# Eight layer normalisations with the sum of squares, root and reciprocal on tokens in the partitions

## What is computed

```python
def layer_norm(x, g=None, b=None):
    x32 = x.astype(jnp.float32)
    mu = jnp.mean(x32, axis=-1, keepdims=True)
    xc = x32 - mu
    y = xc * lax.rsqrt(jnp.mean(xc * xc, axis=-1, keepdims=True) + LN_EPS)
    if g is not None:
        y = y * g + b
    return y.astype(x.dtype)

def first_block(x, c, ...):
    ...
    h = layer_norm(x) * (1.0 + sc_m) + sh_m
    mix = hybrid_mixer(h, ...)
    x = layer_norm(DEEPNORM_ALPHA * x + g_m * mix, ln_mix_g[l], ln_mix_b[l])
    h = layer_norm(x) * (1.0 + sc_f) + sh_f
    ffn = grouped_moe(h, ...)
    x = layer_norm(DEEPNORM_ALPHA * x + g_f * ffn, ln_ffn_g[l], ln_ffn_b[l])

def second_block(x, c, ...):
    for i in range(2):
        ...
        x = layer_norm_2(ALPHA * x + (1.0 + gate) * y, ln_mix_g[i], ln_mix_b[i])
        ...
        x = layer_norm_2(ALPHA * x + (1.0 + gate) * y, ln_ffn_g[i], ln_ffn_b[i])
    return x
```

## Time and profile before

| | us |
|---|---|
| median of three runs | 4085.99 |
| lowest and highest run | 4078.77 and 4087.83 |
| span of the profiled execution | 4087.4 |
| TensorE busy | 3216.4 |
| VectorE busy | 1877.5 |
| ScalarE busy | 885.8 |

### The profile page before, as it was taken

How to read it: one execution, slowest core, us unless ns; L and a number is a source line. 1 busy time by engine, 2 the same in 40 slices (tenths; PEclk the granted TensorE clock), 3 DMA queues, 4 the chain that set the end, 5 groups by cost and what they waited for, 6 DMA issues and landing times. The chain is left out here.

```text
span 4087.4 us, 33743 instructions
## 1 busy us (share of the span) xinstructions
PE 3216.4 (79%) x11149; PEld 1986.0 (49%) x11149; DVE 1877.5 (46%) x2996; ACT 885.8 (22%) x1338; POOL 336.7 (8%) x405
## 2 busy tenths in 40 slices
PE   4699998769988888669995697899843555578998
PEld 3355556544444466434442345678631111257786
DVE  7465463425565524411113444433418888644333
ACT  1211112212222232211112132413210000223132
POOL 0000000000000000010000000000005777000000
PEclk6677678879999988779997788899976777799999
DMA  7453432121111031069883001323020000114220
GB/s 270 124 154 108 123 108 83 61 84 52 35 32 36 0 124 41 1 223 325 311 325 136 28 16 42 124 87 99 21 49 3 0 0 0 41 41 134 93 93 31
DMA packets 305892, 373.55 MB, mean 91 GB/s; under 512 B 31720, under 2 KB 234011, under 8 KB 305820
## 3 DMA queue, kind: packets, MB, share of 16 engines
q1 hardware_dynamic: 298508, 346.92, 26.0%
q0 software_dynamic: 4000, 13.64, 0.9%
q10 hardware_dynamic: 3312, 12.06, 0.7%
HBM read 356.32 MB, written 16.27 MB: 91 GB/s over the span
## 5 line engine op out<-in xcount | busy, mean ns | idle before, releaser
L451 PE MATMUL banks<-mlp_h_parts,mlp_w_parts 128*128 128x512 f32 x1536 | 357.7, 396 | 57.0 <-DVE mlp_w_parts L439 57.0
L451 PEld LDWEIGHTS banks<-mlp_h_parts,mlp_w_parts 128*128 128x128 f32 x1536 | 294.1, 192 | 121.4 <-DVE mlp_w_parts L439 59.5
L451 PE MATMUL banks<-mlp_hidden,mlp_w_parts 128*128 128x512 f32 x1536 | 348.8, 389 | 0.0
L2359 PE MATMUL banks<-h,s_scan_ck 128*32 128x512 f32 x256 | 181.4, 875 | 180.1 <-DVE h L2412 180.1
L451 PEld LDWEIGHTS banks<-mlp_hidden,mlp_w_parts 128*128 128x128 f32 x1536 | 288.3, 188 | 59.8
L439 DVE TENSOR_TENSOR mlp_w_parts<-w_second,mlp_w_parts 128x2048 fp32r<-128x2048 f32 x64 | 146.6, 2293 | 207.1 <-ACT mlp_w_parts L434 207.1
L1641 PE MATMUL banks<-w,experts_xt 128*128 128x512 f32 x544 | 239.0, 598 | 0.9 <-DVE experts_xt L1692 0.9
L2359 PEld LDWEIGHTS banks<-h,s_scan_ck 128*32 128x32 f32 x256 | 36.0, 153 | 324.2 <-DVE h L2412 208.2
L434 ACT ACTIVATE mlp_w_parts<-w_second 128x2048 fp32r<-128x2048 f32 x64 | 122.3, 1913 | 249.0 <-PE banks L451 245.8
L1641 PEld LDWEIGHTS banks<-w,experts_xt 128*128 128x128 f32 x544 | 104.3, 192 | 132.6 <-issue 132.6
L761 DVE SCALAR_TENSOR_TENSOR attention_mod_sum<-w,silu_c,attention_mod_sum 128x256 f32<-128x256 f32 x336 | 162.9, 485 | 12.0
(11 more groups left out here) (550 smaller groups left out, 5148.4 us busy)
## 6 DMA issues: line engine op xcount, KB each, us to landing
w_second<-in_mlp_w_dram SPq DMA_DIRECT2D x64, 1024.0 KB, 5.5
w<-in_w_exp_gate_dram SPq DMA_DIRECT2D x17, 2048.0 KB, 9.4
w<-in_w_exp_up_dram SPq DMA_DIRECT2D x17, 2048.0 KB, 9.2
w<-in_w_exp_down_dram SPq DMA_DIRECT2D x17, 2048.0 KB, 11.0
w<-in_w_ada_dram SPq DMA_DIRECT2D x12, 2048.0 KB, 8.5
w<-in_mod_mix_w_dram SPq DMA_DIRECT2D x24, 1024.0 KB, 9.5
w<-in_mod_ffn_w_dram SPq DMA_DIRECT2D x24, 1024.0 KB, 5.2
w<-in_w_in_dram SPq DMA_DIRECT2D x32, 512.0 KB, 5.5
```

Source lines behind the costliest of these rows:

```text
L451: mm = pe.matmul(out, self.parts[:, n % 2, w, kk, f * P:(f + 1) * P], x[:, v, kk, :], start=(start and kk == 0 and j == 0), stop=(stop and ...
L2359: mm = pe.matmul(ps[rows, 4, :], ck[:, r, 32 * j:32 * j + 32], pr[:, j % 2, n, :], start=(n == 0), stop=(n == 3))
```

## The change

Only `norm_stage` is changed, and with it all eight normalisations. The square tiles become the stationary operand, in blocks of 128 channels by 128 tokens, and one column of ones the moving one. The sum of squares of a token so comes out with tokens on the partitions, one column for each block of 128 tokens, in the banks 1 to 4. Root and reciprocal are taken on 128x4. Four products of 128 columns then bring the result back to the form with tokens in the free dimension and the same value on all partitions: the stationary operand is a column of `rstd` broadcast to 128 columns, the moving one the identity, and the result goes to bank 5, from where VectorE reads it as it scales the tiles. The wait of VectorE for its own reciprocal becomes a wait of TensorE for it (`rstd_done`) and one of VectorE for TensorE (`spread`).

```diff
-    with k.stage(name, "sq_done", "var_done", "std_done", "vec_step", "centred", "scaled", "out_done", "h_done") as (block, s, sb):
+    with k.stage(name, "sq_done", "var_done", "std_done", "rstd_done", "spread", "centred", "scaled", "out_done", "h_done") as (block, s, sb):
...
-        std = sb("std", [P, T])
-        rstd = sb("rstd", [P, T])
+        std = sb("std", [P, TB])
+        rstd = sb("rstd", [P, TB])
...
             for c in range(KD):
                 pe.wait_ge(s["sq_done"], c + 1)
-                mm = pe.matmul(ps[:, 1, :], k.ones[:], sq[:, c, :], start=(c == 0), stop=(c == KD - 1))
+                for b in range(TB):
+                    mm = pe.matmul(ps[:, 1 + b, 0:1], sq[:, c, b * P:(b + 1) * P], k.ones[:, 0:1], start=(c == 0), stop=(c == KD - 1))
             mm.then_inc(s["var_done"], 1)
+            pe.wait_ge(s["rstd_done"], 1)
+            for b in range(TB):
+                mm = pe.matmul(ps[:, 5, b * P:(b + 1) * P], rstd[:, b:b + 1].to_broadcast([P, P]), k.ident[:], start=True, stop=True)
+            mm.then_inc(s["spread"], 1)
             if sum_next:
                 sum_channels(k, pe, lambda c: pe.wait_ge(s["out_done"], c + 1))
...
             dve.wait_ge(s["std_done"], 1)
-            dve.reciprocal(rstd[:], std[:]).then_inc(s["vec_step"], 1)
-            dve.wait_ge(s["vec_step"], 1)
+            dve.reciprocal(rstd[:], std[:]).then_inc(s["rstd_done"], 1)
+            dve.wait_ge(s["spread"], 1)
             for c in range(KD):
-                dve.tensor_tensor(xc[:, c, :], xc[:, c, :], rstd[:], ALU.mult).then_inc(s["scaled"], 1)
+                dve.tensor_tensor(xc[:, c, :], xc[:, c, :], ps[:, 5, :], ALU.mult).then_inc(s["scaled"], 1)
...
             act.wait_ge(s["var_done"], 1)
-            act.activation(std[:], ps[:, 1, :], ACT.Sqrt, scale=1.0 / D, bias=k.eps_ln[:]).then_inc(s["std_done"], 1)
+            act.activation(std[:], ps[:, 1:1 + TB, 0], ACT.Sqrt, scale=1.0 / D, bias=k.eps_ln[:]).then_inc(s["std_done"], 1)
```

## The result

The changed kernel takes 4111.86 us (median of four runs, 4109.22 to 4115.51) against 4086.91 for the kernel before (four runs, 4078.77 to 4088.71). The ratio is 1.0065, with a 95% interval from 1.0051 to 1.0080. It is slower by 25 us, clear of the interval, where the forecast was 26.

The account below looks back on a forecast made before the run. The eight normalisations were taken as chains with nothing beside them. Longer sums less 1.6 us saved behind them gave +3.2 us in seven stages and +3.45 in norm_in, +26 on 4086.0: 4112.0 us, range 4100 to 4127.

Parts of the forecast that it names:

- The chain with nothing beside it: In each of eight normalisations no DMA or other work runs, so a microsecond added or saved there changes the span.
- The sum at the low clock: In norm_in the 64 narrow records of squares stay at clock 0.50 and take 13.95 us, against 8.90 before.
- The clock falls in the seven others: Sums of squares outside norm_in: 0.9 to 3.4 us at the high clock, 2.3 taken, making 12.0 us against 7.18.
- Root, reciprocal and spreading: From root to scaling in each stage: 0.47 plus 2.02, 2.49 us against 4.10, a saving of 1.6.
- Scaling from the banks, and what is queued behind the new wait: VectorE's scaling of tiles does not change; the next sums of channels on TensorE cost or gain nothing.
- The sum: Total over stages: +3.2 us in each of seven, +3.45 in norm_in, together +26 us, 4112.0 us.
- busy TensorE keeps its clock: Rival: narrow products raise and hold the high clock in the sums; -15 us together, 4071 us; chance 5%.
- The late fall to the point of break-even: Rival: high clock lasts about six microseconds in seven stages, which break even; only norm_in pays; 4089 us; chance 4%.
- The dear spreading: Rival: four broadcast operands loaded and streamed in turn, 3.4 us instead of 2.0 in eight stages; 4123 us; chance 9%.

Follow-up runs that it names:

- the rest ahead filled: Changed kernel plus four wide products of the input tiles, into an unread bank, while TensorE rests ahead of the squares: 4108.12 us, ratio 1.0061.
- the second comparison: The changed kernel without an edit, measured once more against the kernel before: 4115.47 us, ratio 1.0079.
- One mixture of wide and narrow products: Changed kernel plus one 512-column product into an unread bank for each tile of squares: 4136.68 us, ratio 1.0135 to the kernel before.

## Why the prediction was right

Its number came out at 4112.0 against 4111.86, and its mechanism is the one that the runs show. Two of its terms were too small, by 3 us together, and that the number met all the same is chance.

- *The chain with nothing beside it.* Right. The stages got longer by what their own steps did.
- *The sum at the low clock, 13.95 us.* 13.85 in norm_in, with a clock of 0.50 throughout. The router and the one-column sums of the modulation were the right rows.
- *The clock falls in the seven others, 0.9 to 3.4 us after the start.* Right in kind, and confirmed with the rest ahead filled. The time at the high level was over-sized: it was 1.7 us in the mean of the seven, where I had 2.3, and the sums took 12.33 us where I had 12.0. norm_mix with its 0.5 us lies outside my bounds. A small error went the other way. From record to record it is 0.112 us at the high clock and 0.213 at the low one, in the change and in the attention's 24 as well; my 0.117 came from the whole length of those 24, of which the last already runs at the low clock. With 0.112 some 15 records are cheap, 0.102 us each, and the sum comes to 12.3. I had taken the delays of the fall from stretches in which TensorE rested, counted from its last wide product.
- *Root, reciprocal and spreading, 2.49 us.* 2.64. The root on 128x4 was the mis-sized term with 0.26 us against 0.20, and the spreading with its hand-over took 2.11 or 2.12 against 2.02. The reciprocal's 0.18 was right. The broadcast operand loads at the same 0.213 us a record as a plain one at this clock; all eight records last 2.08 us where the plain ones lasted 1.97.
- *Scaling from the banks, and what is queued behind the new wait.* The scaling did not change, as said: the tiles take 4.87 us for eight in norm_in. The sums of channels that follow in norm_mix, which I had put at nothing, start as long after the first scaled tile as before, but take 8.75 us instead of 9.40, since the clock rises 3.3 us after their start and not 4.6. That is 0.65 us of the 6 that the stages don't account for.
- *The sum.* By the stages +3.7 us in seven, where I had +3.2, and +3.5 in norm_in: 29 us. The profile shows 6 of them taken back where no line was changed, the medians show 25, and the second comparison 28.7. The intervals of the two comparisons are 21 to 33 us and 27 to 38, and both hold the 29 of the stages. So the forecast of 26 is some 3 us too low, and that 4112.0 met 4111.86 is luck.
- *The rivals.* That busy TensorE keeps its clock, and would make the change faster at 4071 us, is refuted in eight stages and again with the rest filled. The late fall to the point of break-even did not occur either: the longest high stretch was some 3 us of the 6 it needed. The dear spreading did not occur: 2.08 us, and not 3.4. The Trainium skill, "TensorE: Matmul & The Clock Gate", in its table "Why this matters for your kernels", advises to keep TensorE busy without a break to get past the low clock. Read by busy time, this does not hold for these products: norm_in's 13.8 us of them, busy throughout, stay at 0.50.

## What to carry to other kernels

Count the loads of the stationary operand before turning a sum around. A product with one moving column costs its load, 0.112 us a record at the high clock and 0.213 at the low, and a float32 one costs two records. For one tile of 512 tokens that is eight narrow records, 0.90 us at the high clock and 1.71 at the low; two wide ones of 512 columns cost 0.86 at the high clock. Look for what the new instructions do to TensorE's clock as well as for their own price: here it cost some 4.8 us of the sum in each of seven stages (12.3 measured against 7.5, an estimate from 64 records at 0.112 us and 0.4 behind them), and another 0.9 us of the products behind it in all eight. By that estimate the change would have been faster than the kernel before if its seven stages had kept the high clock; no run shows it. A small root and reciprocal can be had without a narrow sum, if the wide result is turned once at its end.

## What the runs showed that I had not expected

- The moment at which the clock falls repeats. In two executions of the changed kernel the eight sums agree within 0.13 us, although norm_mix starts 2 us later in one of them. Between kernels the moment differs: in norm_mix 0.5 us into the narrow products of the change, and 5 us with the rest filled. Why the fall comes at these moments stays open.
- One mixture of wide and narrow products holds 1.00 where it starts at 1.00 (14.1 us) and stays at 0.50 where it starts there (27.4 us).
- Wide products alone are not enough. Eight records of 512 columns with gaps between them let the clock fall where sixteen without a gap held it.
